# Cache passes of a hybrid attention step share their row buffers, and each asks at its end for the first rows and bias of the next

## What is computed

```python
def mix(qd, q_pos, kd, k_pos, win_kv, win_pos, rel_bias):
    o_sb = stick_breaking(qd['sb_q'], kd['sb_k'], kd['sb_v'], q_pos, k_pos)          # 4 heads, own keys
    o_dsa = dsa_attention(..., kd['idx_k'], q_pos, k_pos, rel_bias[:, :H_DSA])        # top 256 keys by index score
    o_nsa = nsa_attention(..., rel_bias[:, H_DSA:])                                   # compressed, selected, window
    ...
def sample_layer(x, c_sb, c_dsa, c_idx, c_nsa, s_win, page_table, ...):
    def with_past(cache, new):
        past = cache[page_table].reshape(bsz, -1, *cache.shape[2:])
        return jnp.concatenate([past, new.astype(past.dtype)], axis=1)
```

## Time and profile before

| | us |
|---|---|
| median of 3 runs | 2785.68 (2782.86 to 2787.16) |
| the profiled execution | 2777.18 |
| its span, first to last instruction | 2775.4 |
| PE, DVE, ACT, POOL busy | 2328.8, 1019.1, 757.6, 492.2 |

### The profile page before, as it was taken

The page is one execution under the profiler, slowest core; times in us unless marked ns, Lnnn a source line. Parts: engine busy times, 40 slices in busy tenths (PEclk is TensorE's granted clock), DMA queues, the critical chain, the costliest instruction groups (busy, mean ns, idle before and its releaser), DMA issues. The chain is left out here.

```text
span 2775.4 us, 45204 instructions
## 1 busy us (share of the span) xinstructions
PE 2328.8 (84%) x16097; PEld 1765.4 (64%) x16097; DVE 1019.1 (37%) x1707; ACT 757.6 (27%) x1706; POOL 492.2 (18%) x337
## 2 busy tenths in 40 slices
PE   5999999999976999995588778887499756798996
PEld 3888888888875999993255444444255433576885
DVE  5111101010001222222368856766333227997213
ACT  4000000000011222220044444445255336554010
POOL 6433333333223000000000000000000000244331
PEclk7999999999988999996899979999699867999998
DMA  5323233323348787633499699999599663003223
GB/s 184 123 93 125 93 108 110 105 104 107 141 124 236 246 245 227 206 100 72 110 338 356 245 370 386 383 383 374 153 363 380 230 223 99 1 1 111 87 84 114
DMA packets 344410, 522.91 MB, mean 188 GB/s; under 512 B 67501, under 2 KB 150846, under 8 KB 341902
## 3 DMA queue, kind: packets, MB, share of 16 engines
q1 hardware_dynamic: 309722, 483.10, 51.4%
q10 hardware_dynamic: 31792, 32.05, 3.8%
q0 software_dynamic: 2704, 5.33, 0.6%
HBM read 498.09 MB, written 44.00 MB: 195 GB/s over the span
## 5 line engine op out<-in xcount | busy, mean ns | idle before, releaser
L461 PE MATMUL proj_acc<-proj_w_hi,h_hi 128*128 128x512 f32 (+1 forms) x960 | 369.9, 385 | 8.5 <-POOL proj_w_lo L430 8.5
L462 PE MATMUL proj_acc<-proj_w_hi,h_lo 128*128 128x512 f32 (+1 forms) x960 | 370.1, 386 | 0.0
L463 PE MATMUL proj_acc<-proj_w_lo,h_hi 128*128 128x512 f32 (+1 forms) x960 | 369.4, 385 | 0.0
L430 POOL TENSOR_TENSOR proj_w_lo<-w_in,proj_w_hi 128x2048 fp32r<-128x2048 f32 (+1 forms) x60 | 272.6, 4546 | 459.2 <-DVE proj_w_hi L399 459.2
L754 PE MATMUL cmp_hp<-cmp_xT,cmp_w 128*128 128x128 f32 x2048 | 251.6, 277 | 12.2 <-DVE cmp_xT L785 12.2
L399 DVE CAST proj_w_hi<-w_in 128x2048 fp32r<-128x2048 f32 (+1 forms) x60 | 80.8, 1350 | 466.5 <-PE proj_acc L454 463.7
L754 PEld LDWEIGHTS cmp_hp<-cmp_xT,cmp_w 128*128 128x128 f32 x2048 | 239.4, 193 | 16.3 <-DVE cmp_xT L785 15.8
L485 ACT COPY proj_out<-proj_acc 128x512 f32<-128x512 f32 (+1 forms) x60 | 34.6, 577 | 697.3 <-PE proj_acc L463 697.3
L1250 PE MATMUL sb_tp<-kept_consts,sb_k_rows 128*128 128x128 f32 x1024 | 165.2, 309 | 68.8 <-DMA sb_k_rows<-in_cache_sb_kv_dram 50.4
L1250 PEld LDWEIGHTS sb_tp<-kept_consts,sb_k_rows 128*128 128x128 f32 x1024 | 123.5, 155 | 141.6 <-DMA sb_k_rows<-in_cache_sb_kv_dram 63.6
L461 PEld LDWEIGHTS proj_acc<-proj_w_hi,h_hi 128*128 128x128 f32 x960 | 180.7, 188 | 44.3 <-issue 8.8
(11 more groups left out here) (407 smaller groups left out, 3477.8 us busy)
## 6 DMA issues: line engine op xcount, KB each, us to landing
cmp_rows<-in_cache_nsa_kv_dram SPq DMA_DIRECT2D x512, 128.0 KB, 2.3
slc_rows<-in_cache_nsa_kv_dram SPq DMA_DIRECT2D x256, 256.0 KB, 4.9
sb_k_rows<-in_cache_sb_kv_dram SPq DMA_DIRECT2D x256, 256.0 KB, 6.0
sb_v_rows<-in_cache_sb_kv_dram SPq DMA_DIRECT2D x256, 256.0 KB, 6.9
dsa_rows<-in_cache_dsa_kv_dram SPq DMA_DIRECT2D x256, 256.0 KB, 4.7
w_in<-in_w_in_dram SPq DMA_DIRECT2D x56, 1024.0 KB, 4.8
fin_w<-in_w_out_dram SPq DMA_DIRECT2D x32, 512.0 KB
proj<-proj_out ACTq DMA_DIRECT2D x14, 1024.0 KB, 4.3
```

The lines of the kernel that those rows point to most:

```text
L430: pool.tensor_tensor(w_lo[q][:, :, 0:width], w[q][:, :, 0:width], w_hi[q][:, :, 0:width], ALU.subtract).then_inc(lo_made, 1)
L461: pe.matmul(to, h_hi[:, kk, r], w_hi[q][:, k, 0:width], start=(kk == 0), stop=False)
L462: pe.matmul(to, h_lo[:, kk, r], w_hi[q][:, k, 0:width], start=False, stop=False)
L463: last = pe.matmul(to, h_hi[:, kk, r], w_lo[q][:, k, 0:width], start=False, stop=(kk == KT_IN - 1))
```

## The change

Four row buffers of 16 KB a partition, `kept.rows`, and semaphores for them (`kept.arrived`) now live through all four passes. slc and dsa use them as their 4 slots and win as 3 (it had 2). sb's key ring lies in the first three (`key_place`), and two of its value pieces in the fourth. Each pass ends, on SP, with the first loads of the pass behind it (`ahead`), each behind a wait for its place (`free`): `index_scores` asks for slc's steps 0 to 2, slc for sb's 6 key pieces, sb for dsa's steps 0 to 2, and dsa for win's.

The biases come early too: slc's is loaded by SP in `index_scores` after chunk 0. dsa's is split into `bias_lo` (2048 columns and the 8 new ones), loaded at sb's end, and `bias_hi`, loaded by ACT at dsa's start; DVE waits for `bias_hi` at step 4.

```diff
+AHEAD = 3
+RING = 6
+def step_rows(sp, nc, io, kept, tag, cache, col, n, free):
+    g, c = divmod(n, NCH)
+    free(n)
+    pages = page_numbers(nc, io, kept.paired, g * (2 * NPG) + c * (2 * PPC), 2 * PPC)
+    for b in range(2):
+        to = kept.rows[n % 4][:].rearrange("p (b m c) -> p b m c", b=2, m=PPC)[:, b]
+        load_pages(sp, pages[b * PPC:(b + 1) * PPC], to, cache, col, 4 * DH, kept.arrived[tag][n % 4][b])
+def key_place(kept, m):
+    return kept.rows[m % RING // 2][:, m % 2 * 2048:(m % 2 + 1) * 2048].rearrange("p (m c) -> p m c", m=PPC)
...
@@ index_scores, SP and POOL
                 load(sp, mybir.EngineType.SP, 0, c)
+                if c == 0:
+                    sp.wait_ge(bias_zeroed, 1)
+                    load_bias(sp, io, kept.bias_nsa, 6, 0, kept.bias_nsa_in)
+            for n in range(AHEAD):
+                step_rows(sp, nc, io, kept, "slc", io.nsa_cache, 512, n, lambda n: None)
+            pool.memset(kept.bias_nsa, 0.0).then_inc(bias_zeroed, 1)
...
@@ stream
-    SLOTS = 2 if stick or nch == 1 else 4
+    SLOTS = 2 if stick else 3 if nch == 1 else 4
...
+                    if n < ready:
+                        continue
                     new_values_used(i)
...
-                keys_of(0, 0, pages, range(per))
                 for n, (g, c) in enumerate(steps):
                     more = n + 1 < len(steps)
                     if more:
                         next_pages = pages_of(*steps[n + 1])
-                        keys_of(*steps[n + 1], next_pages, range(ahead))
+                        if n:
+                            keys_of(*steps[n + 1], next_pages, range(spare))
                     values_of(g, c, pages)
...
+            def free(n):
+                if stick:
+                    steps_done, b = divmod(groups * nch * per - RING + 2 * n + 1, per)
+                    sp.wait_ge(k_turned, SLOTS * items + steps_done * items + (heads - 1) * per + b + 1)
+                else:
+                    sp.wait_ge(v_used, SLOTS * per + (groups * nch - 4 + n + 1) * per)
+            if ahead is not None:
+                ahead(sp, free)
...
-                act.wait_ge(zeroed, len(new_biases[:1]) + 1)
-                load_biases(act, new_biases[:1], bias_in)
+                if late is not None:
+                    act.wait_ge(zeroed, 1)
+                    load_bias(act, io, late[0], late[2], late[1], late_in)
+                act.wait_ge(zeroed, 1 + (late is not None))
...
+                if late is not None and n * CH == late[1]:
+                    dve.wait_ge(late_in, 16 * items)
...
@@ stick_breaking
+    def ahead(sp, free):
+        sp.wait_ge(kept.bias_lo_zeroed, 1)
+        load_bias(sp, io, kept.bias_lo[:, 0:PAST // 2], 0, 0, kept.bias_lo_in)
+        load_bias(sp, io, kept.bias_lo[:, PAST // 2:], 0, PAST, kept.bias_lo_in)
+        for n in (2, 0, 1):
+            step_rows(sp, nc, io, kept, "dsa", io.dsa_cache, 0, n, lambda n: free((n + 1) % 3))
@@ dsa_sample
+    def ahead(sp, free):
+        for g in range(AHEAD):
+            free(g)
+            for b in range(2):
...
+                sp.dma_start(to, io.win_state[g * 2 + b].rearrange("(m p) c -> p m c", p=P)).then_inc(kept.arrived["win"][g][b], 64)
@@ slc_sample
+    def ahead(sp, free):
+        for m in range(RING):
+            n, b = divmod(m, 4)
+            if m % 2 == 0:
+                free(m // 2)
+            if b == 0:
+                pages = page_numbers(nc, io, kept.by_chunk, (NCH - 1 - n) * (NB * PPC), 4 * PPC)
+            load_pages(sp, pages[b * PPC:(b + 1) * PPC], key_place(kept, m), io.sb_cache, 0, 4 * DH, kept.arrived["sb"][m])
```

More of the change, by code:

```diff
@@ L527, in load_pages, with load_bias @@
         sp.dma_start(to[:, p], src).then_inc(sem, 16)
+AHEAD = 3
[9 more added lines that the diff above has]
+    return kept.rows[m % RING // 2][:, m % 2 * 2048:(m % 2 + 1) * 2048].rearrange("p (m c) -> p m c", m=PPC)
+def load_bias(eng, io, to, first, col, sem):
+    for j in range(4):
+        h = first + j % 2 * 3
+        eng.dma_start(to[j * 32:j * 32 + 24, :], io.token_lines[h:h + 3, :, col:col + to.shape[1]].rearrange("h t k -> (h t) k")).then_inc(sem, 16)
 def compress(nc, io, kept):
@@ L1135, in data, with mask_new @@
             return nch - 1 - c if stick else c
-        def load_biases(eng, biases, sem):
-            for to, first in biases:
-                for j in range(items):
-                    h = first + j % heads * 3
-                    eng.dma_start(to[j * rise:j * rise + 24, :], io.token_lines[h:h + 3, :, KEYS - to.shape[1]:].rearrange("h t k -> (h t) k")).then_inc(sem, 16)
-        def mask_new(to):
-            last = slice(to.shape[1] - NT, to.shape[1])
-            return nc.vector.tensor_tensor(to[:, last], to[:, last], kept.consts[:, C_NM:C_NM + NT], ALU.add)
+        def mask_new(new):
+            return nc.vector.tensor_tensor(new, new, kept.consts[:, C_NM:C_NM + NT], ALU.add)
         @block.sync
@@ L1239, in turn @@
                     m = n * per + b
-                    here = k_ring[m % RING]
+                    here = key_place(kept, m)
                     if h == 0:
@@ L1489, in limit @@
                 at = parity(g, c)
-                here = slice(data(c) * CH, (data(c) + 1) * CH)
+                here = bias(data(c) * CH, (data(c) + 1) * CH)
                 one = lambda x, k: x[:, bass.ds(g, 1), k:k + 1].rearrange("p o k -> p (o k)")
@@ L1635, in keys, with bias @@
         return kept.drop[:, PAST:KEYS] if c is None else kept.drop[:, c * CH:(c + 1) * CH]
+    def bias(lo, hi):
+        if lo >= PAST:
+            return kept.bias_lo[:, PAST // 2 + lo - PAST:PAST // 2 + hi - PAST]
+        return kept.bias_lo[:, lo:hi] if hi <= PAST // 2 else kept.bias_hi[:, lo - PAST // 2:hi - PAST // 2]
+    def ahead(sp, free):
+        for g in range(AHEAD):
+            free(g)
+            for b in range(2):
+                to = kept.rows[g][:].rearrange("p (b m c) -> p b m c", b=2, m=PPC)[:, b]
+                sp.dma_start(to, io.win_state[g * 2 + b].rearrange("(m p) c -> p m c", p=P)).then_inc(kept.arrived["win"][g][b], 64)
     stream(nc, io, kept, "dsa", cache=io.dsa_cache, col=0, proj_v=DSA_V, heads=2, per=2, q=kept.q_dsa, k_new=kept.k_dsa,
-           select=kept.sel_d, dropped_keys=keys, bias=kept.bias_dsa, new_biases=((kept.bias_dsa, 0), (kept.bias_win, 6)), head0=4)
+           select=kept.sel_d, dropped_keys=keys, bias=bias, bias_in=(kept.bias_lo_in, 128), late=(kept.bias_hi[:], PAST // 2, 0),
+           extra=((kept.bias_win, 6),), ahead=ahead, head0=4)
 def cmp_sample(nc, io, kept):
@@ L2528, in program @@
             kept.top8 = sample.sb("top8", [NS, 8])
+            kept.rows = [sample.sb(f"rows{i}", [P, 4096]) for i in range(4)]
+            kept.bias_lo = sample.sb("bias_lo", [P, PAST // 2 + NT])
+            kept.bias_lo_zeroed, kept.bias_lo_in, kept.bias_nsa_in = sample.sem("bias_lo_zeroed"), sample.sem("bias_lo_in"), sample.sem("bias_nsa_in")
+            kept.arrived = {tag: [[sample.sem(f"{tag}_in{i}_{b}") for b in range(2)] for i in range(n)] for tag, n in (("slc", 4), ("dsa", 4), ("win", 3))}
+            kept.arrived["sb"] = [sample.sem(f"sb_in{i}") for i in range(RING)]
             with nc.sbuf_tensor("scores", [NS, KEYS], F32) as kept.scores:
-                index_scores(nc, io, kept)
                 with nc.sbuf_tensor("bias_nsa", [P, KEYS], F32) as bias_nsa:
                     kept.bias_nsa = bias_nsa[:]
+                    index_scores(nc, io, kept)
                     slc_sample(nc, io, kept)
                 stick_breaking(nc, io, kept)
-            with nc.sbuf_tensor("bias_dsa", [P, KEYS], F32) as bias_dsa:
-                kept.bias_dsa = bias_dsa[:]
+            with nc.sbuf_tensor("bias_hi", [P, PAST // 2], F32) as kept.bias_hi:
                 dsa_sample(nc, io, kept)
```

81 lines of the change are left out of this document (45 added, 36 removed).

## The result

| | before | changed |
|---|---|---|
| median | 2786.34 us (2782.86 to 2787.16, 4 runs) | 2719.20 us (2717.38 to 2723.03, 4 runs) |
| ratio to before, 95% interval | | 0.9762 [0.9748, 0.9776] |
| profiled execution, its span | 2777.18, 2775.4 | 2723.03, 2721.2 |

Twelve more runs were made. The ratio of each is to runs of the kernel before that were measured beside it, whose medians lie between 2784.3 and 2787.7 us; so kernels of different experiments are compared by their ratios and passes. One execution of "changed again" (3893 us) and one of "before, three slots in win" (3078 us), both at a lower granted clock, are left out of the ratios. The profiles of the twelve, and those of the two above, give this table of the passes, from the first instruction of one to that of the next, in us. Each kernel is explained at its experiment.

The account below looks back on a forecast made before the run. It took sb as bound by transfers, slc by PE and engines it trades with, with standstills between passes. Terms 18 + 11 + 17.4 + 15.4 = 61.8 us off 2785.7 gave a median of 2724, range 2709 to 2745.

Parts of the forecast that it names:

- The sum: All passes: gains of 18, 11, 17.4 and 15.4 us, together 61.8, giving a median of 2724 us.
- Start of slc: First exponential about 1368.9 instead of 1388.82 as the bias is already loaded: 19.9 us go, net 18.
- slots 0 to 2 are full: At slc's first transpose, rows of three slots are already loaded, so PE's pace of some 5.9 us a step follows.
- The index pass: Ahead of slc: SP's added row loads end near 1367, charged 2 us; nothing charged for the bias transfer.
- the bias load stretches the index pass: Rival, index pass: the bias load takes 17.95 us and delays SP's queue, 10 us lost, 2734; chance 0.15.
- Start of sb: Six key pieces loaded during the end of slc: 11 us go, bounds 0 and 16.3.
- the two key pieces then land near 1622: Start of sb: the last key pieces of step 1 arrive near 1622, where the last came at 1633.64 before.
- Start of dsa: With the bias split and its low half early, the exponential comes by about 1986.3 instead of 2003.69: 17.4 us go.
- win: Three of win's four steps are asked for at the end of dsa, only step 3 waits: 15.4 us go.
- sb isn't sped up: Rival, sb: DVE's top 8 rounds or SP's stop eat the head start, 11 us missing, 2735; chance 0.15.
- Slower: Rival, sb: SP's stop recurs every step, DMA idles 7.7 us in 15 steps, 116 us, 2851; chance 0.03.
- It doesn't do what it says: Rival, pass ends: SP reaches its early requests only when the pass is over, nothing won, 2786; chance 0.03.

Follow-up runs that it names:

- changed again: The changed kernel, no edit, run again for a second profile: 2718.8 us, ratio to before 0.9763.
- before, three slots in win: The kernel before with three row slots in win instead of two, nothing else: 2773.3 us, ratio to before 0.9956.
- Biases early only: The changed kernel, but no pass asks for rows of the next one; biases still come early: 2737.8 us, ratio to before 0.9828.
- rows early only: The changed kernel, but ACT asks for the biases of slc and dsa at the pass start; rows still early: 2732.7 us, ratio to before 0.9814.
- shared buffers only: The changed kernel with neither rows nor biases asked for early, buffers still shared: 2756.0 us, ratio to before 0.9897.
- experiment 2: The changed kernel, but sb asks for its own first six key pieces instead of slc: 2725.2 us, ratio to before 0.9782.
- experiment 8: The changed kernel with slc's bias asked for behind SP's last index load instead of behind chunk 0: 2722.3 us, ratio to before 0.9776.
- Both of these: The changed kernel with slc's bias behind the last index load and sb's step 1 values ahead of its seventh key piece: 2727.0 us, 0.9791.

## Why the prediction came out right, step by step

*The sum* was 61.8 us, the medians differ by 67.1. For a profiled execution I had 2715; the first was 2723.0, 7.0 us of it behind win, and the second 2716.5. That the sum came so near is in part luck: the terms for the index pass and for win hold for other reasons than I gave, and in sb an effect that I didn't know of fills the gap that a mis-sized term leaves.

*Start of slc, 19.9:* 19.7 at the first transpose. Right, and by its mechanism. That DMA had to be free as well ("slots 0 to 2 are full") matters less here than in dsa: 3.7 us of the 18.5.

*The index pass, 2:* 2.4 in the first profile and 3.4 in the second ones. The size was near and the step wrong. I charged SP's tail of 24 row loads and took nothing for the transfer of the bias "since DMA is half idle there". "Biases early only" has no tail and costs 3.2 to 3.9 us, "rows early only" has the tail and costs nothing. That is counted from the kernel before. Counted from "shared buffers only" (92.3, one profile) the tail costs 2.2 us, the bias 6.1 and both 5.4 to 5.6, and some of it is paid by a pass that became shorter for a reason that wasn't tried. The rival "the bias load stretches the index pass" had the right mechanism and three times the size (10 us): it let everything behind the bias wait for the 17.95 us that it took at the start of slc. Here PE waits 7.03 us for the rows behind it, and its wait for ACT shrinks from 7.81 to 3.54.

*Start of sb, 11:* 7.3. The gap of DMA came as said, and SP went on within 0.1 us of the time that I worked out. The step that failed is "the two key pieces then land near 1622": I counted two pieces at full rate from SP's first request, 5.4 us, and left out the time from a request to its first bytes and the slower start behind it (299 GB/s from 1605 to 1610). From 1602.87 to the use of the second piece at 1611.91 it is 9.0 us, and with 9.0 in place of 5.4 my 11 us become 7.4 to 8. The other 7 to 8 us of sb come from where the buffers lie. The prediction had the rest of sb "bound by DMA at the same rate", and the rate wasn't the same.

*Start of dsa, 17.4:* 17.1. The sum holds, with a part that I had hidden in it. I priced only the wait for the bias; without the early rows 6.2 us of it would have come back as a wait for rows.

*win, 15.4:* 16.7, and the wait "near 6 us" is 2.00. The step took the early request for the cause. The third slot does 13 to 14 us of it without any request in another pass, since step 2 then waits for nothing. The last wait is short since step 3's rows are asked for at 2167.25, at the start of step 2's turns: its first half is used 5.7 us later, as I said, but PE has work until then.

*The rivals.* "sb isn't sped up" is out by experiment 2. "Slower" had the stop recur in every step: SP's longest stop behind the start is 4.0 us, and DMA is at 1.03 to 1.05 from there to 1880. "It doesn't do what it says" is out by SP's row loads at 1354.98, within the index pass.

## What to carry to other kernels

When a change shares buffers in order to load ahead, run the sharing alone: here it gave nearly half of the gain. The slot and the addresses that came with it made up 21 to 22 us, about a third of the whole gain, and each can be had by a line. In a part bound by transfers, look at where the destination buffers begin before the order of loads; a pad of 32 bytes was worth as much as the whole rearrangement of sb. Behind a full ring, the one other order that was tried only moved the gap of DMA and recovered none of it.

## What the runs showed of the hardware

- The rate of loads from HBM into SBUF with 2 KB rows depended on the start of the destination in the partition: 384 to 386 GB/s at 32 bytes past a multiple of 64, 388 at 192 past a multiple of 256, 405 at multiples of 256, at a DMA share of 1.05 or 1.06 each time. The share doesn't show it.
- A load of 24-row pieces (1.58 MB in all, with 144 packets) holds the DMA engines out of proportion: with row loads beside it the share is 0.92 to 0.96 at 127 to 179 GB/s (experiment 8), where rows alone move 384 to 405 at 1.05.
- The part behind win takes 523.0 to 530.8 us with the same code. Between the two profiles of the changed kernel the difference goes with PE's granted clock 50 to 100 us into it: the first stretch below is the changed kernel's first profile. At 0.57 more of the stretch goes at 1.2 GHz than at 0.70, and PE does less in it (104 matmuls in 30.66 us against 115 in 25.11).

```profile
2240.39:2290.39 50.00, 30.66 (x104) 17.38 (x103) 29.18 (x41) 25.89 (x49) 0.92 (x6) 0.57 0.29 83
```

And the second:

```profile
2241.50:2291.50 50.00, 25.11 (x115) 14.87 (x114) 36.56 (x58) 29.09 (x58) 0.92 (x6) 0.70 0.28 83
```

So a difference of 5 us between two of these kernels can come from a part that neither touched, and the table by pass tells more than the medians. "Both of these" has 0.69 in this stretch and 527.7 us all the same, so this stretch isn't all of it. Why the clock rises later in some of them was not tried.
